# Expert loop written out without branches, and ScalarE issuing the down weights

## The chip, the cores and the metric

The kernel is one program on one core of one Trainium2 chip. The metric is the device time of one execution in microseconds (us), the median of repeated executions. The program is written instruction by instruction for each engine: TensorE (PE in the profile, PEld for its weight loads), VectorE (DVE), ScalarE (ACT), GpSimd (POOL) and SyncE (SP, which issues most transfers). Engines wait for each other and for transfers through semaphores.

## The reference, cut to what matters

A hybrid layer over 512 tokens of width 1024: a mixer (gated linear attention and dilated attention), a router, and a mixture of 32 experts, four for each token. The change touches the experts only:

```python
def expert_block(args):
    xb, e = args
    h = xb @ w_gate_up[e] + b_gate_up[e]
    gate = jnp.minimum(h[:, ::2], SWIGLU_LIMIT)
    up = jnp.clip(h[:, 1::2], -SWIGLU_LIMIT, SWIGLU_LIMIT)
    act = (up + 1.0) * (gate * jax.nn.sigmoid(SWIGLU_ALPHA * gate))
    return act @ w_down[e] + b_down[e]
```

`w_gate_up[e]` is 1024 x 2048 and `w_down[e]` is 1024 x 1024, both in float32: 8 MiB and 4 MiB for each expert, 384 MiB for all 32. The result is weighted by the router's gate, added up per token, and followed by an RMS norm.

## The kernel before, in words

The mixer and the router come first (up to about 672 us). Then the expert stage begins, the method `experts`. Each expert's weights are read once, as 12 chunks of 1 MiB: 8 chunks of gate and up weights (q = 0 to 7), then 4 chunks of down weights (q = 8 to 11). The chunks lie in a ring of 16 buffers (`expert_chunk` and `expert_chunk_late` in the trace). Chunk c goes to buffer c % 16, and it is issued once chunk c - 16 has been used up: PE adds 1 to the semaphore `used` after each chunk, and the issuing engine waits for `used` >= c - 15. PE waits for a chunk's own semaphore before it multiplies (`chunk_here`, L1745).

The stage works in bodies. Body e does, in this order on PE: the gate/up products of expert e+1 (8 chunks, L1915), with the turning (transposing) of expert e's activations after chunks 2 and 3 (L1888), and then the down products of expert e (4 chunks, L1924), with the turning of the gathered rows of expert e+2 (L1878) and its bias products (L1908) after the second of them. While PE does the down products, VectorE makes the activations of expert e+1 from PSUM (`swiglu`, L2001 to L2011) and ScalarE the sigmoid (L1972). ScalarE also copies turned rows and activations back (L1895, L1900), and at the end of a body writes the weighted output rows (`rows_out`, L1981). GpSimd scatters those rows to memory with an adding indirect DMA (L1870) and gathers the rows of expert e+2 (L1796). The output rows wait for the scatter of the body before.

There are 31 bodies (e = 0 to 30). Two stand before a hardware loop, 28 are in it (7 turns of 4 bodies), and one stands after it. Every engine runs this same structure:

```python
        def over_bodies(engine, body):
            for e0 in range(PEELED):
                body(engine, e0, 0)
            with engine.Fori(0, TURNS) as i:
                for u in range(self.UNROLL):
                    body(engine, PEELED + u, i)
            for e0 in range(PEELED + self.UNROLL * TURNS, LAST):
                body(engine, e0, 0)
```

A turn of the loop has 48 chunks, three times around the ring; semaphore targets and expert numbers in the loop are computed from the turn's number. SyncE issues all 12 chunks of each body in order (`load_chunk`, L1743), and after the first down chunk the three small transfers of a later expert's bias rows (L1737). After the last body, PE does the down products of expert 31 on their own (L1932), whose chunks are 380 to 383.

Of the kernel before, what the change touches and what calls it, by code (L numbers as in the profile page):

```python
# [9 lines left out]
F32R = mybir.dt.float32r  # L10
I32 = mybir.dt.int32
# [5 lines left out]
P = 128  # L17
# [29 lines left out]
N_EXPERTS, TOP_K, FF = 32, 4, D_MODEL  # L47
# [79 lines left out]
class Kernel:  # L127
# [23 lines left out]
    def build(self):  # L151
        nc = self.nc
        with ExitStack() as top:
# [33 lines left out]
            with ExitStack() as late:  # L187
# [7 lines left out]
                with ExitStack() as moe:  # L195
# [11 lines left out]
                    first = [self.sb(moe, f"expert_chunk{j}", [P, 2, self.WIDE]) for j in range(self.GU)]  # L207
# [13 lines left out]
                    self.bias_place = self.sb(moe, "bias_place_r", [P, P], F32R)  # L221
                    self.index = [self.sb(moe, f"row_index{u}", [P, 1], I32) for u in range(self.UNROLL)]
                    self.piece_row = [self.sb(moe, f"piece_row{u}", [P, self.GROUPS], I32) for u in range(self.UNROLL)]
                    self.piece_weight = [self.sb(moe, f"piece_weight{u}", [P, self.GROUPS]) for u in range(self.UNROLL)]
                    self.moe = {n: self.sem("moe_" + n) for n in (
# [1489 lines left out]
    RING = 16  # L1715
    GU, PER_BODY, UNROLL = 8, 12, 4
    PER_TURN = PER_BODY * UNROLL
    PARTS, GROUPS = P // QUARTER, FIRST_SLOTS // QUARTER
# [102 lines left out]
    def experts(self, stack):  # L1821
        nc, t = self.nc, self.t
        E, GU, BODY, TURN, RING = N_EXPERTS, self.GU, self.PER_BODY, self.PER_TURN, self.RING
        G, PARTS, PIECE, Q = self.GROUPS, self.PARTS, self.PIECE, QUARTER
# [79 lines left out]

        def gate_up_bias(pe, e0, i=0):
            pe.wait_ge(self.bias_in[e0 % 2], 16 * G * (self.UNROLL // 2) * i + 16 * G * (e0 // 2 + 1))
            for j, bank in enumerate(h_banks):
                pe.matmul(bank, self.bias_place[part_rows(j), :], self.bias_rows[e0 % 2][part_rows(j), :].bitcast(F32R),  # L1908
                          start=True, stop=False)

        def gate_up_chunk(pe, c, i, k, x=xT):
            w = chunk_here(pe, c, i)
# [6 lines left out]
        def down_chunk(pe, c, i, q):  # L1919
            w = chunk_here(pe, c, i)  # L1920
# [14 lines left out]

        def body_pe(pe, e0, i):
            e, more = i * self.UNROLL + e0, e0 < E - 2
            for q in range(BODY):
                c = self.body_chunk(e0, q)
                if q == 0:  # L1940
                    pe.wait_ge(S["x_out"], 2 * e + 4)
                    if e0 == 0:
                        pe.wait_ge(S["gu"], 2)
                        gate_up_bias(pe, 1)
                if q < GU:
                    gate_up_chunk(pe, c, i, q)
                else:
                    if q == GU:
                        pe.wait_ge(S["aT_out"], G * e + G)
                        if e0:  # L1950
                            pe.wait_ge(S["y_out"], G * e)
                    if q == BODY - 2 and e0 == E - 2:
                        turn_act(pe, E - 1, range(2))
                    if q == BODY - 1 and e0 == E - 2:
                        turn_act(pe, E - 1, range(2, G))
                    down_chunk(pe, c, i, q - GU)
                if q == 2:
                    turn_act(pe, e, range(2))
                if q == 3:
                    turn_act(pe, e, range(2, G))  # L1960
                if q == 9 and more:
                    turn_rows(pe, e + 2)
                    pe.wait_ge(S["gu"], 2 * e + 4)
                    gate_up_bias(pe, e0 + 2, i)

# [7 lines left out]

        def rows_out(act, e0, i):
            e = i * self.UNROLL + e0
            act.wait_ge(S["used"], TURN * i + self.body_chunk(e0, BODY - 1) + 1)
            act.wait_ge(S["pieces"], 2 * e + 2)
            if e0:
                act.wait_ge(S["scattered"], 16 * G * e)
            for j in range(G):  # L1980
                act.activation(y[:, j * PIECE:(j + 1) * PIECE], y_of(j), ACT.Copy,  # L1981
                               scale=self.piece_weight[e0 % self.UNROLL][:, j:j + 1]).then_inc(S["y_out"], 1)
# [13 lines left out]
        def swiglu(dve, e, c, i, first=False):  # L1996
            dve.wait_ge(S["used"], TURN * i + c + 1)
            if not first:
# [13 lines left out]

        def body_dve(dve, e0, i):
            e, more = i * self.UNROLL + e0, e0 < E - 2
            if more:
                u = (e0 + 2) % self.UNROLL
                if e0 > 1:
# [5 lines left out]
            swiglu(dve, e + 1, self.body_chunk(e0, GU - 1), i)  # L2023

# [45 lines left out]

        with nc.Block() as block:
            @block.sync
            def _(sp):
# [8 lines left out]

                def body(sp, e0, i):
                    e = i * self.UNROLL + e0
                    for q in range(BODY):
                        c = self.body_chunk(e0, q)
# [29 lines left out]
            def _(pool):  # L2116
# [20 lines left out]

                def body(pool, e0, i):
                    e = i * self.UNROLL + e0
                    if e0 < E - 2:  # L2140
                        gather(pool, e + 2, (e0 + 2) % self.UNROLL)
                    scatter(pool, e, e0 % self.UNROLL)
                over_bodies(pool, body)
# [29 lines left out]
            def _(dve):  # L2173
# [4 lines left out]
                dve.wait_ge(self.normed_stored, 16 * NB)  # L2178
                swiglu(dve, 0, GU - 1, 0, first=True)
                dve.wait_ge(S["lists_in"], 16 * (1 + PARTS))  # L2180
# [36 lines left out]
            def _(pe):  # L2217
# [9 lines left out]
                for c in range(GU):  # L2227
                    gate_up_chunk(pe, c, 0, c, as_rows(aT))
                    if c == 5:
# [288 lines left out]
```

## Time and profile before

| what | us |
|---|---|
| median of 3 runs | 1821.0 (1819.9 to 1821.1) |
| profiled execution, its own time | 1832.81 |
| span of the profiled execution | 1831.0 |
| PE busy in that span | 1767.4 (97%) |
| VectorE, ScalarE, GpSimd busy | 449.8, 378.9, 218.1 |
| one body without a pause (881.02 to 914.60) | 33.58 |

The profiled execution is 11.8 us longer than the median run, so a sum made from the trace is set against 1832.81 first and brought to the median afterwards. A row of the timeline gives the start, the time of the whole group, the engine and line, what is written from what, how many records, and in brackets how long the engine was idle before it and what ended that. "issue" means that the profile shows nothing the engine waited for.

### The profile page before, as it was taken

To read this page: it belongs to the slowest core of one execution; us is meant where nothing else is said; L and a number is where in the kernel's file an instruction comes from. 1 tells how busy PE (TensorE), PEld (TensorE's weight loads), DVE (VectorE), ACT (ScalarE), POOL (GpSimd) and SP (SyncE) were. 2 spreads that over 40 slices of the span, in tenths; PEclk is the share of its full clock that TensorE was granted. 3 is DMA by queue.
4 is the path that set the end of the run, shared out by engine and by line. 5 is a ranking of instruction groups with operands and counts; after the bars stand their busy time and mean duration, and the time that the engine had idled before them with its cause. 6 is when DMAs were issued, how large, how long until landed. Compare 5 with 4: busy or idle time off the path is not lost.

```text
span 1831.0 us, 38017 instructions
## 1 busy us (share of the span) xinstructions
PE 1767.4 (97%) x16447; PEld 996.1 (54%) x16448; DVE 449.8 (25%) x692; ACT 378.9 (21%) x673; POOL 218.1 (12%) x182
## 2 busy tenths in 40 slices
PE   9999999999999989999999989989999989989997
PEld 7877788898888863433433433434334334334433
DVE  4256255446324540100100100100010001001003
ACT  4254232246422321110101111111111101101111
POOL 1000000000000013121112112112111211211111
PEclk9999999999999989999999999999999999999999
DMA  5321344412223787999989999999999999999973
GB/s 186 123 92 47 120 139 116 122 40 100 92 92 138 270 329 288 384 388 398 394 321 395 394 338 386 397 334 375 397 347 389 389 343 381 392 344 382 397 276 100
DMA packets 112158, 500.47 MB, mean 273 GB/s; under 512 B 19512, under 2 KB 29712, under 8 KB 62400
## 3 DMA queue, kind: packets, MB, share of 16 engines
q1 hardware_dynamic: 92272, 479.12, 68.4%
q0 software_dynamic: 18672, 16.74, 4.5%
q10 hardware_dynamic: 1056, 2.16, 0.5%
q8 instruction: 140, 2.29, 0.5%
q14 instruction: 18, 0.15, 0.0%
HBM read 486.07 MB, written 21.15 MB: 277 GB/s over the span
## 4 chain that ended last, share of the span: by engine, by line
PE 61%; issue 2%; DVE 0%; POOL 0%; ACT 0%; DVEq 0%
PE psum L1915 38%; PE psum L1924 18%; PE psum L1888 2%; PE psum L1878 1%; PE psum L1908 1%; PE psum L1932 1%; PE psum L244 0%; DVE expert_chunk L2056 0%; DVE h_sb L2212 0%; POOL total_rstd L2147 0%; PE psum L2045 0%; PE psum L2039 0%; ACT up_values L2168 0%; DVE gate_values L2212 0%; PE psum L2237 0%
## 5 line engine op out<-in xcount | busy, mean ns | idle before, releaser
L1915 PE MATMUL psum<-expert_chunk,rowsT 128*32 128x512 f32 x2976 | 341.9, 611 | 30.7 <-issue 30.7
L1915 PE MATMUL psum<-expert_chunk_late,rowsT 128*32 128x512 f32 x2976 | 328.5, 593 | 0.0
L2001 DVE TENSOR_SCALAR gate_values<-psum 128x768 f32<-128x768 f32 x32 | 30.6, 958 | 974.9 <-PE psum L1915 974.9
L1870 POOL DMA_INDIRECT residual_rows<-h_sb,piece_row x93 | 145.4, 1564 | 903.9 <-ACT h_sb L1981 830.0
L1915 PEld LDWEIGHTS psum<-expert_chunk,rowsT 128*32 128x32 f32 x2976 | 97.1, 112 | 243.9 <-issue 242.2
L1915 PEld LDWEIGHTS psum<-expert_chunk_late,rowsT 128*32 128x32 f32 x2976 | 93.4, 110 | 202.9 <-issue 200.5
L290 DVE TENSOR_TENSOR chunk_lo<-chunk,chunk_hi 128x2048 fp32r<-128x2048 f32 x48 | 110.0, 2291 | 257.5 <-ACT chunk_hi L286 238.7
L1924 PE MATMUL psum<-expert_chunk_late,activationsT 128*32 128x256 f32 x3072 | 172.2, 380 | 0.0
L1924 PE MATMUL psum<-expert_chunk,activationsT 128*32 128x256 f32 x2880 | 161.3, 380 | 0.0
L321 PE MATMUL psum<-xT_hi,chunk_hi 128*128 128x512 f32 x384 | 150.3, 392 | 4.5 <-DVE chunk_lo L290 2.0
L321 PE MATMUL psum<-xT_hi,chunk_lo 128*128 128x512 f32 x384 | 149.5, 389 | 0.0
L321 PE MATMUL psum<-xT_lo,chunk_hi 128*128 128x512 f32 x384 | 149.5, 389 | 0.0
L1924 PEld LDWEIGHTS psum<-expert_chunk_late,activationsT 128*32 128x32 f32 x3072 | 98.1, 110 | 73.8 <-issue 13.6
L286 ACT CAST chunk_hi<-chunk 128x2048 fp32r<-128x2048 f32 x48 | 91.8, 1913 | 189.5 <-PE psum L321 158.0
L1924 PEld LDWEIGHTS psum<-expert_chunk,activationsT 128*32 128x32 f32 x2880 | 92.1, 110 | 69.3 <-issue 12.6
L321 PE MATMUL psum<-chunk_hi,xT_hi 128*128 128x512 f32 x288 | 113.5, 394 | 2.6 <-ACT gla_v L723 1.5
L321 PE MATMUL psum<-chunk_hi,xT_lo 128*128 128x512 f32 x288 | 112.7, 391 | 0.0
L321 PE MATMUL psum<-chunk_lo,xT_hi 128*128 128x512 f32 x288 | 112.6, 391 | 0.0
L1900 ACT COPY activationsT<-psum 128x256 f32<-128x256 f32 x93 | 31.6, 374 | 338.6 <-PE psum L1888 305.0
L1972 ACT ACTIVATE gate_sigmoid<-gate_values 128x768 f32<-128x768 f32 x32 | 27.1, 847 | 350.0 <-DVE gate_values L2001 350.0
L321 PEld LDWEIGHTS psum<-xT_hi,chunk_hi 128*128 128x128 f32 x384 | 72.1, 188 | 21.3 <-DVE chunk_lo L290 2.7
L321 PEld LDWEIGHTS psum<-xT_hi,chunk_lo 128*128 128x128 f32 x384 | 72.1, 188 | 15.2
(281 smaller groups left out, 1533.1 us busy)
## 6 DMA issues: line engine op xcount, KB each, us to landing
expert_chunk<-in_expert_w_gate_up SPq DMA_DIRECT2D x132, 1024.0 KB
expert_chunk_late<-in_expert_w_gate_up SPq DMA_DIRECT2D x124, 1024.0 KB, 8.3
expert_chunk_late<-in_expert_w_down SPq DMA_DIRECT2D x68, 1024.0 KB, 8.1
expert_chunk<-in_expert_w_down SPq DMA_DIRECT2D x60, 1024.0 KB
chunk<-in_w_in SPq DMA_DIRECT2D x38, 1024.0 KB, 5.1
chunk<-in_w_branch_gla SPq DMA_DIRECT2D x4, 1024.0 KB, 5.1
chunk<-in_w_mix_out SPq DMA_DIRECT2D x4, 1024.0 KB, 5.1
gla_v<-in_x SPq DMA_DIRECT2D x4, 512.0 KB
```

The source lines that it names most:

```text
L286: act.copy(self.whi[c][:], self.raw[c][:]).then_inc(self.hi_done[c], 1)
L290: dve.tensor_tensor(self.wlo[c][:], self.raw[c][:], self.whi[c][:].bitcast(F32), ALU.subtract).then_inc(self.lo_done[c], 1)
L321: last = pe.matmul(bank, stationary, moving, start=(k == 0 and n == 0), stop=(k == KT - 1 and n == 2))
L1870: pool.indirect_dma_start(pieces, bass.IndirectOffsetOnAxis(ap=self.piece_row[u][:, j:j + 1], axis=0), y[:, j * PIECE:(j + 1) * PIECE], No ...
L1878: last = pe.transpose(turned(f)[:, k, :], rows[taken, (HALF_KT * f + k) * P:(HALF_KT * f + k + 1) * P], self.ident[taken, taken])
L1888: last = pe.transpose(turned_act(j)[:, k * P:(k + 1) * P], a[:, (2 * j + k) * P:(2 * j + k + 1) * P], self.ident[:])
L1900: act.copy(dst[:, :, :, part_rows(j)].rearrange("p q k r -> p k q r"), turned_act(j).rearrange("p (k q r) -> p k q r", k=2, q=PARTS)).then ...
L1908: pe.matmul(bank, self.bias_place[part_rows(j), :], self.bias_rows[e0 % 2][part_rows(j), :].bitcast(F32R), start=True, stop=False)
L1915: last = pe.matmul(bank[part_rows(p), :], x[:, k, part_rows(j)], w[:, p // 2, p % 2 * COLS:(p % 2 + 1) * COLS], start=False, stop=(k == KT ...
L1924: last = pe.matmul(y_of(j)[part_rows(p), :], aT[:, q, kk, part_rows(j)], w[:, kk, p * PIECE:(p + 1) * PIECE], start=(q == 0 and kk == 0), ...
L1972: act.activation(sg[:, 0:HELD], gv[:, 0:HELD], ACT.Sigmoid, scale=SWIGLU_ALPHA).then_inc(S["sig"], 1)
L2001: dve.tensor_scalar(by_row(gv), gates_ups[:, :, :, :, 0], SWIGLU_LIMIT, None, ALU.min).then_inc(S["gu"], 1)
```

## The change

The loop over the bodies is written out for all engines: no loop instruction, no branch, and all semaphore targets and expert numbers are constants. Four buffers of the small index tables stay four. In addition, the down chunks of each expert but expert 0 are issued by ScalarE, in its own DMA queue, instead of SyncE: in body e ScalarE issues the four down chunks of expert e+1, after the sigmoid of expert e+1 and before it copies the turned rows back. The four waits for free ring buffers are kept, before each transfer. SyncE keeps the gate/up chunks, the bias rows and the four down chunks of expert 0.

```diff
-    def chunk_here(self, pe, c, i=0):
-        pe.wait_ge(self.chunk_loaded[c % self.RING], 16 * (self.PER_TURN // self.RING) * i + 16 * (c // self.RING + 1))
+    def chunk_here(self, pe, c):
+        pe.wait_ge(self.chunk_loaded[c % self.RING], 16 * (c // self.RING + 1))
         return self.expert_ring[c % self.RING]
...
-        def body_act(act, e0, i):
-            e = i * self.UNROLL + e0
+        def body_act(act, e):
             act_back(act, e, aT)
             gate_sigmoid(act, e + 1)
-            if e0 < E - 2:
+            for q in range(BODY - GU):
+                c = self.body_chunk(e + 1, GU + q if e + 1 < LAST else q)
+                act.wait_ge(S["used"], c - RING + 1)
+                self.load_down(act, c, e + 1, q)
+            if e < E - 2:
                 rows_back(act, e + 2, xT)
             else:
                 act_back(act, E - 1, as_act(xT))
-            rows_out(act, e0, i)
+            rows_out(act, e)
...
-        PEELED, LAST = 2, E - 1
-        TURNS = (LAST - PEELED) // self.UNROLL
+        LAST = E - 1
 
         def over_bodies(engine, body):
-            for e0 in range(PEELED):
-                body(engine, e0, 0)
-            with engine.Fori(0, TURNS) as i:
-                for u in range(self.UNROLL):
-                    body(engine, PEELED + u, i)
-            for e0 in range(PEELED + self.UNROLL * TURNS, LAST):
-                body(engine, e0, 0)
+            for e in range(LAST):
+                body(engine, e)
...
-                def body(sp, e0, i):
-                    e = i * self.UNROLL + e0
+                def body(sp, e):
                     for q in range(BODY):
-                        c = self.body_chunk(e0, q)
-                        if c < RING:
-                            continue
-                        sp.wait_ge(S["used"], TURN * i + c - RING + 1)
-                        if q < GU:
-                            self.load_gate_up(sp, c, e + 1, q)
-                        else:
-                            self.load_down(sp, c, e, q - GU)
-                        if q == GU and e0 < E - 2:
-                            self.load_bias_rows(sp, e + 2, e0)
+                        c = self.body_chunk(e, q)
+                        if c >= RING and (q < GU or e == 0):
+                            sp.wait_ge(S["used"], c - RING + 1)
+                            if q < GU:
+                                self.load_gate_up(sp, c, e + 1, q)
+                            else:
+                                self.load_down(sp, c, e, q - GU)
+                        if q == GU and e < E - 2:
+                            self.load_bias_rows(sp, e + 2, e)
                 over_bodies(sp, body)
-                for q in range(4):
-                    c = self.body_chunk(LAST, q)
-                    sp.wait_ge(S["used"], c - RING + 1)
-                    self.load_down(sp, c, LAST, q)
```

The other bodies (`body_pe`, `body_dve`, GpSimd's) lose the turn's number in the same way and keep their instructions and their order.

## Rows read from the trace of the kernel before

**Rows 1.** The page, part 1: busy time, share of the span, instructions.

```profile
PE 1767.4 (97%) x16447; PEld 996.1 (54%) x16448; DVE 449.8 (25%) x692; ACT 378.9 (21%) x673; POOL 218.1 (12%) x182
```

**Rows 2.** Waits of PE, 713 to 1800 us: total, times, longest.

```profile
PE psum L1915 <- issue: 30.7, 7, 6.3
```

**Rows 3.** Timeline of PE around the loop's turns.

```profile
780.30 7.91 PE L1915 MATMUL psum<-expert_chunk,rowsT 128*32 128x512 f32 x72
788.14 0.66 PE L1888 MATMUL psum<-identity_sb,h_sb 128*128 128x128 f32 x4
...
909.39 5.39 PE L1924 MATMUL psum<-expert_chunk_late,activationsT 128*32 128x256 f32 x96
919.84 10.63 PE L1915 MATMUL psum<-expert_chunk,rowsT 128*32 128x512 f32 x72 [5.06 <-issue]
...
1638.90 0.66 PE L1888 MATMUL psum<-identity_sb,h_sb 128*128 128x128 f32 x4
...
1765.34 7.91 PE L1915 MATMUL psum<-expert_chunk,rowsT 128*32 128x512 f32 x72
1773.18 0.66 PE L1888 MATMUL psum<-identity_sb,h_sb 128*128 128x128 f32 x4
```

**Rows 4.** Windows: busy us (records) of each engine, granted clock, DMA share, GB/s.

```profile
919.84:930.40 10.56, 10.56 (x73) 2.75 (x73) 0.00 (x0) 0.00 (x0) 3.28 (x3) 0.74 0.64 172
```

**Rows 5.** The same view, one body without a pause, one with it, one late.

```profile
881.02:914.60 33.58, 33.58 (x405) 13.54 (x397) 3.95 (x7) 3.93 (x9) 5.75 (x4) 1.00 1.01 388
914.60:948.20 33.60, 28.54 (x274) 9.54 (x274) 3.30 (x4) 3.07 (x7) 5.75 (x4) 0.90 0.87 304
...
1698.20:1731.77 33.57, 33.57 (x405) 13.67 (x401) 3.95 (x7) 3.93 (x9) 5.75 (x4) 1.00 1.02 399
```

**Rows 6.** DMA queues, 914 to 926 us: packets, MB, share of 16 engines.

```profile
q8 instruction: 3, 0.05, 1.6%
```

**Rows 7.** DMA queues, 1117 to 1130 us.

```profile
q8 instruction: 1, 0.02, 0.5%
q0 software_dynamic: 6, 0.00, 0.0%
```

**Rows 8.** Waits of SP's queue, 713 to 1800 us.

```profile
SPq L1743 <- PE psum L1915: 521.5, 236, 10.6
SPq L1743 <- PE psum L1924: 282.2, 120, 3.6
```

**Rows 9.** Chunks of expert_chunk_late, 748 to 781 us: issue to landing.

```profile
DMA to landing us min/median/max: 8.6/8.7/8.9
```

**Rows 10.** The same, 882 to 910 us.

```profile
DMA to landing us min/median/max: 8.4/8.5/8.6
```

**Rows 11.** Timeline of all engines in one body, 1100 to 1140 us.

```profile
1111.87 0.33 SPq L1743 DMA_DIRECT2D expert_chunk<-in_expert_w_down  x1
...
1120.46 0.84 ACT L1972 ACTIVATE gate_sigmoid<-gate_values 128x768 f32<-128x768 f32 x1 [11.09 <-DVE gate_values L2001]
...
1125.09 0.86 ACT L1895 COPY rowsT<-psum 128x384 f32<-128x384 f32 x2 [3.79 <-PE psum L1878]
...
1130.95 7.91 PE L1915 MATMUL psum<-expert_chunk_late,rowsT 128*32 128x512 f32 x72
```

**Rows 12.** DMA instructions in ScalarE's queue (L1110): count, duration ns min/median/max.

```profile
L1110 ACTq DMA_DIRECT2D qk_halves_then_probsT<-att_kT x16: 631/672/769, 304.6 to 331.3; - x16
L1110 ACTq DMA_DIRECT2D qk_halves_then_probsT<-att_qT_window x8: 632/1131/1732, 215.7 to 223.9; - x8
```

**Rows 13.** Timeline of PE, 1620 to 1831 us: the end of the stage.

```profile
1798.88 13.97 PE L1932 MATMUL psum<-expert_chunk_late,rowsT 128*96 128x512 f32 x32
```

**Rows 14.** Timeline of ACT, 1720 to 1831 us.

```profile
1788.42 0.85 ACT L1972 ACTIVATE gate_sigmoid<-gate_values 128x768 f32<-128x768 f32 x1 [11.09 <-DVE gate_values L2001]
1792.94 0.65 ACT L1900 COPY rowsT<-psum 128x256 f32<-128x256 f32 x2 [3.67 <-PE psum L1888]
```

**Rows 15.** DMA issues by line: count, KB each, median us to landing.

```profile
chunk<-in_w_in SPq DMA_DIRECT2D x38, 1024.0 KB, 5.1
```

More of the change, by code:

```diff
@@ L221, in build @@
                     self.bias_place = self.sb(moe, "bias_place_r", [P, P], F32R)
-                    self.index = [self.sb(moe, f"row_index{u}", [P, 1], I32) for u in range(self.UNROLL)]
-                    self.piece_row = [self.sb(moe, f"piece_row{u}", [P, self.GROUPS], I32) for u in range(self.UNROLL)]
-                    self.piece_weight = [self.sb(moe, f"piece_weight{u}", [P, self.GROUPS]) for u in range(self.UNROLL)]
+                    self.index = [self.sb(moe, f"row_index{u}", [P, 1], I32) for u in range(self.BUFFERS)]
+                    self.piece_row = [self.sb(moe, f"piece_row{u}", [P, self.GROUPS], I32) for u in range(self.BUFFERS)]
+                    self.piece_weight = [self.sb(moe, f"piece_weight{u}", [P, self.GROUPS]) for u in range(self.BUFFERS)]
                     self.moe = {n: self.sem("moe_" + n) for n in (
@@ L1715 @@
     RING = 16
-    GU, PER_BODY, UNROLL = 8, 12, 4
-    PER_TURN = PER_BODY * UNROLL
+    GU, PER_BODY, BUFFERS = 8, 12, 4
     PARTS, GROUPS = P // QUARTER, FIRST_SLOTS // QUARTER
@@ L1901, in act_back, with gate_up_bias, gate_up_chunk @@
                          turned_act(j).rearrange("p (k q r) -> p k q r", k=2, q=PARTS)).then_inc(S["aT_out"], 1)
-        def gate_up_bias(pe, e0, i=0):
-            pe.wait_ge(self.bias_in[e0 % 2], 16 * G * (self.UNROLL // 2) * i + 16 * G * (e0 // 2 + 1))
+        def gate_up_bias(pe, e):
+            pe.wait_ge(self.bias_in[e % 2], 16 * G * (e // 2 + 1))
             for j, bank in enumerate(h_banks):
-                pe.matmul(bank, self.bias_place[part_rows(j), :], self.bias_rows[e0 % 2][part_rows(j), :].bitcast(F32R),
+                pe.matmul(bank, self.bias_place[part_rows(j), :], self.bias_rows[e % 2][part_rows(j), :].bitcast(F32R),
                           start=True, stop=False)
-        def gate_up_chunk(pe, c, i, k, x=xT):
-            w = chunk_here(pe, c, i)
+        def gate_up_chunk(pe, c, k, x=xT):
+            w = chunk_here(pe, c)
             for j, bank in enumerate(h_banks):
@@ L1917, in gate_up_chunk, with down_chunk @@
             last.then_inc(S["used"], 1)
-        def down_chunk(pe, c, i, q):
-            w = chunk_here(pe, c, i)
+        def down_chunk(pe, c, q):
+            w = chunk_here(pe, c)
             for kk in range(2):
@@ L1934, in last_down_chunk, with body_pe @@
             last.then_inc(S["used"], 1)
-        def body_pe(pe, e0, i):
-            e, more = i * self.UNROLL + e0, e0 < E - 2
+        def body_pe(pe, e):
+            more = e < E - 2
             for q in range(BODY):
-                c = self.body_chunk(e0, q)
+                c = self.body_chunk(e, q)
                 if q == 0:
                     pe.wait_ge(S["x_out"], 2 * e + 4)
-                    if e0 == 0:
+                    if e == 0:
                         pe.wait_ge(S["gu"], 2)
@@ L1945, in body_pe @@
                 if q < GU:
-                    gate_up_chunk(pe, c, i, q)
+                    gate_up_chunk(pe, c, q)
                 else:
@@ L1949, in body_pe @@
                         pe.wait_ge(S["aT_out"], G * e + G)
-                        if e0:
+                        if e:
                             pe.wait_ge(S["y_out"], G * e)
-                    if q == BODY - 2 and e0 == E - 2:
+                    if q == BODY - 2 and e == E - 2:
                         turn_act(pe, E - 1, range(2))
-                    if q == BODY - 1 and e0 == E - 2:
+                    if q == BODY - 1 and e == E - 2:
                         turn_act(pe, E - 1, range(2, G))
-                    down_chunk(pe, c, i, q - GU)
+                    down_chunk(pe, c, q - GU)
                 if q == 2:
@@ L1963, in body_pe @@
                     pe.wait_ge(S["gu"], 2 * e + 4)
-                    gate_up_bias(pe, e0 + 2, i)
+                    gate_up_bias(pe, e + 2)
         def gate_sigmoid(act, e, first=False):
@@ L1972, in gate_sigmoid, with rows_out @@
             act.activation(sg[:, 0:HELD], gv[:, 0:HELD], ACT.Sigmoid, scale=SWIGLU_ALPHA).then_inc(S["sig"], 1)
-        def rows_out(act, e0, i):
-            e = i * self.UNROLL + e0
-            act.wait_ge(S["used"], TURN * i + self.body_chunk(e0, BODY - 1) + 1)
+        def rows_out(act, e):
+            act.wait_ge(S["used"], self.body_chunk(e, BODY - 1) + 1)
             act.wait_ge(S["pieces"], 2 * e + 2)
-            if e0:
+            if e:
                 act.wait_ge(S["scattered"], 16 * G * e)
@@ L1991, in body_act, with swiglu @@
                 act_back(act, E - 1, as_act(xT))
-            rows_out(act, e0, i)
-        def swiglu(dve, e, c, i, first=False):
-            dve.wait_ge(S["used"], TURN * i + c + 1)
+            rows_out(act, e)
+        def swiglu(dve, e, c, first=False):
+            dve.wait_ge(S["used"], c + 1)
             if not first:
@@ L2011, in swiglu, with body_dve @@
             dve.tensor_tensor(a[:, 0:HELD], uv[:, 0:HELD], sg[:, 0:HELD], ALU.mult).then_inc(S["act"], 1)
-        def body_dve(dve, e0, i):
-            e, more = i * self.UNROLL + e0, e0 < E - 2
+        def body_dve(dve, e):
+            more = e < E - 2
             if more:
-                u = (e0 + 2) % self.UNROLL
-                if e0 > 1:
+                u = (e + 2) % self.BUFFERS
+                if e > 1:
                     dve.wait_ge(S["scattered"], 16 * G * (e - 1))
@@ L2022, in body_dve @@
                 list_hot(dve, E - 1)
-            swiglu(dve, e + 1, self.body_chunk(e0, GU - 1), i)
+            swiglu(dve, e + 1, self.body_chunk(e, GU - 1))
         def further_experts(dve):
@@ L2136, in _, with body @@
                                    ).then_inc(S["lists_in"], 16)
[L2138 to L2142, printed above, removed]
+                def body(pool, e):
+                    if e < E - 2:
+                        gather(pool, e + 2, (e + 2) % self.BUFFERS)
+                    scatter(pool, e, e % self.BUFFERS)
                 over_bodies(pool, body)
@@ L2178, in _ @@
                 dve.wait_ge(self.normed_stored, 16 * NB)
-                swiglu(dve, 0, GU - 1, 0, first=True)
+                swiglu(dve, 0, GU - 1, first=True)
                 dve.wait_ge(S["lists_in"], 16 * (1 + PARTS))
@@ L2227, in _ @@
                 for c in range(GU):
-                    gate_up_chunk(pe, c, 0, c, as_rows(aT))
+                    gate_up_chunk(pe, c, c, as_rows(aT))
                     if c == 5:
```

7 lines of the change are left out of this document (3 added, 4 removed).

## The prediction

> **What bounds the kernel now.** I read the page first: PE is busy 97% of the span [rows 1], so only PE's idle time and slow time are to be won. The list of PE's waits over the expert stage then shows what there is: 30.7 us in seven waits, all before L1915 and all put down to "issue", a wait for nothing the profile shows [rows 2]. The timeline of PE says where. A body starts at 780.30 with no idle time, but the first products of the second turn start 5.06 us after the end of the last ones, and 72 products then take 10.63 us where 7.91 is normal [rows 3]. The granted clock in those 10.56 us is 0.74, a mix of 2.4 and 1.2 GHz, and it is 1.00 in a body without a pause [rows 4, 5]. PE had been idle just before. The pauses lie at the six returns from the end of the loop to its start. The first entry (780.30) and the exit (body 30, at 1765.34) have none [rows 3].
>
> Price of the pauses: the turning at L1888 in the first body of a turn is at 788.14 in the first turn and at 1638.90 in the seventh, 850.76 us later. Without a return, four bodies take 1773.18 - 1638.90 = 134.28 us, 33.57 each [rows 3]. Six turns at that pace are 805.68. The rest, **45.08 us**, is 7.5 for each return: 30.7 idle [rows 2], 14.4 in slow products.
>
> Next I asked whether transfers would take over. In bodies without a pause the DMA share is 1.01 to 1.02 at 388 to 399 GB/s; in the one with a pause 0.87 at 304 [rows 5]. So the transfer engines are full too, and get a rest only in the pauses. But SP waits before its chunk transfers, 356 times, 804 us in all, for PE to free a buffer [rows 8]; PE's seven waits were all at the returns. And the time from issue to landing doesn't grow from one body to those some 130 us later in the same turn: 8.7, then 8.5 us [rows 9, 10]. A need above 33.57 us of transfer for each body would add up there. PE bounds, transfers come within about 1%.
>
> **The loop written out.** PE keeps every product and order; only the returns go. What is left between two bodies is what stands between the bodies inside a turn: nothing. The terms are -30.7 idle, and -14.4 for the clock, since PE is no longer idle before it. Sum -45.1. All other engines lose their returns too; they wait for PE, so 0. The constants in place of registers on SP save nothing, as SP waits for PE anyway [rows 8].
>
> The mechanism I assume is fetching instructions: three packets of the instruction queue in the 12 us around a return, against one in 13 us in mid-body [rows 6, 7]. Written out, PE reads the same number of instructions in sequence, as it does inside a turn, which is 134 us without a pause. "Advanced Engine Details and Errata" of the Trainium skill, section Control Flow Timing, gives a jump 51 ns and a compare-and-jump 108 ns: by it six returns would cost 0.65 us at most and the time would be about 1820.4. "Runtime: NRT & Kernel Launch" of the Trainium skill, section Instruction fetch mechanics, says that a taken branch out of a small window must first fetch its target. The traced 5 us idle speaks for the second page.
>
> **ScalarE's transfers.** Four DMA instructions a body enter between the sigmoid, which ends at 1121.30, and the copy of the turned rows at 1125.09, before which ScalarE is idle 3.79 us [rows 11]. The nearest rows for one such instruction in its queue are 0.672 us (median) and, at worst, 1.73 [rows 12]. Four take 2.7 us: hidden in the 3.79. At the worst they take 6.9: the copy then ends at 1129.1, and PE needs it at 1130.95 [rows 11]. The four waits for `used` ask for chunks 4 to 7 of the body, which the sigmoid's own wait already implies, so they hold nothing up: 0. In the last body the sigmoid ends at 1789.27 and the next copy starts at 1792.94 [rows 14]: 2.7 fits, 6.9 is 3.3 too late. So 0, with +3.3 as the other end; the median row is nearest.
>
> **Later transfers.** The first of the four was issued at 1111.87 [rows 11] and will be at 1121.3: 9.4 us later, the others less. A chunk is issued 15 chunks of PE work ahead of its use, 15/12 x 33.57 = 42.0 us. Less 8.7 of landing [rows 9] and 9.4 of lateness leaves 24 us. The four come in one burst while SP goes on with its own; the work for the transfer engines stays the same, so they stay busy on a backlog instead of an even stream: 0. The gather that PE's turning waits for is over by 1117 [rows 7], ahead of the burst: 0. SP's bias transfers go out a few us sooner: 0.
>
> The last expert's down chunks are special: SP has them long ready, now they are issued from 1789.3 on. PE wants the first at 1798.88 and one every 13.97/4 = 3.5 us [rows 13]. Other chunks are done by then, so landing takes between 5.1 us, a lone chunk in the mixer [rows 15], and 8.7 [rows 9]: with 0.7 for the instruction, 1795.1 to 1798.7. Each further MiB at 390 GB/s is 2.7 us, faster than PE. So 0; with an instruction of 1.73 us and the long landing, +0.9.
>
> **Sum.** Against the profiled execution's own time: 1832.81 - 45.1 = 1787.7. Its distance of 11.8 us to the median isn't placed by any row; I let it stay: 1821.0 - 45.1 = **1776**. If all 11.8 us sat in the pauses, unprofiled runs would lose only 33.3 and come to 1787.7.
>
> **Rivals.**
>
> *Transfers become the bound, in part.* For: the share of 1.02, no rest any more, two hardware queues at once for over 1000 us, which no row shows. Against: no growth of landing in four bodies. If two queues served together raise a body's need by x us over 33.57, the 24 us of lead are eaten first, then PE waits: 31x - 24. At x = 1.5 (throughput down 4%) this is 22.5 us lost and 1798.
>
> *Transfers bound it outright (the slow side).* Same place, larger x: at 31x - 24 = 45, x = 2.2, a loss of 6% in GB/s, the gain is gone. At 10% a body needs 37.3 us: 91.6 lost, 1867. "DMA: Bandwidth & Descriptors" of the Trainium skill, section Queues, rings and completion order, says that each transfer engine takes turns between the queues that have work, a packet at a time; by it throughput would hold, and only the chunks would land in another order. No row here shows two loaded hardware queues.
>
> *The pause isn't the jump's.* Something else that comes each fourth body, such as the ring's third time around, stays: 1821. Against: no pause at the entry nor at the exit.
>
> *The pauses are shorter without a profile:* 1783 to 1788, as above.
>
> **How the numbers follow.** Forecast as worked out, 1770 to 1783: 0.64. Pauses shorter, 1783 to 1788: 0.10. Transfers in part, 1776 to 1818: 0.14, half of it above 1797. Not the jump: 0.04. Slow side: 0.08. The range 1769 to 1797 leaves out 0.07 + 0.04 + 0.08 = 0.19; its low end allows for some us of gain from code that lies differently in memory, as no row excludes it. The measurement can tell about 0.2% from no change. Faster is 0.64 + 0.10 + 0.14 = 0.88, same 0.04, slower 0.08.
>
> **What would show it.** Right: PE has no idle time of over 1 us between two bodies from 713 us to the last, 33.57 us for each of them, granted clock 1.00, and the stage ends 45 us sooner. ScalarE's DMA instructions total under 3.8 us a body, and its copy of rows still waits for PE. Landing times rise from 8.5 us toward 15 for chunks that meet a burst, and SP still waits for PE. Wrong: pauses of PE at chunk waits, at q = 8 or in gate/up chunks of late experts, with GB/s below 388 in full windows; or "issue" pauses that come back in written-out code; or a wait of PE before L1932 for the last four chunks.

## Result and the profile after

The changed kernel takes 1778.9 us (median of 4 runs, 1778.25 to 1779.55), the kernel before 1820.45 (1819.14 to 1821.1): a ratio of 0.9773, 95% interval 0.9756 to 0.979. That is 41.6 us less; 45.1 less and 1776 were forecast. A later comparison (experiment 10) gave 1778.6 against 1821.9, ratio 0.9761 (0.9747 to 0.9774). The profiled execution took 1779.54 us, with a span of 1777.7.

The page of the kernel after: lines of parts 1, 3 and 5 (the costliest product groups). They answer to [rows 1] and [rows 2]. Lines moved by one or two: L1914 is the gate/up product, L1923 the down product, L1887 the turning of activations, L1742 the chunk transfer.

```profile
span 1777.7 us, 36227 instructions
PE 1748.5 (98%) x16447; PEld 991.6 (56%) x16448; DVE 449.9 (25%) x692; ACT 379.0 (21%) x673; POOL 218.2 (12%) x182
...
q1 hardware_dynamic: 74416, 349.09, 50.4%
q10 hardware_dynamic: 18912, 132.20, 18.8%
...
L1914 PE MATMUL psum<-expert_chunk,rowsT 128*32 128x512 f32 x2976 | 328.6, 593 | 0.0
L1914 PE MATMUL psum<-expert_chunk_late,rowsT 128*32 128x512 f32 x2976 | 328.5, 593 | 0.0
```

From the page of the kernel before:

```profile
q10 hardware_dynamic: 1056, 2.16, 0.5%
...
L1915 PE MATMUL psum<-expert_chunk,rowsT 128*32 128x512 f32 x2976 | 341.9, 611 | 30.7 <-issue 30.7
```

PE has the same number of products as before. The 30.7 us of idle time before L1914 are now 0.0. The group that starts each turn of the loop, on `expert_chunk`, lost 13.3 us of busy time (341.9 before, 328.6 now) and is as fast as its twin on the late buffers. Queue q10 is ScalarE's: it carries 132 MB where it carried 2.16 before, and q1 carries 130 MB less.

The timeline of PE in the kernel after, from the first expert to the last products of the stage. It answers to [rows 3] and [rows 13].

```profile
687.39 7.93 PE L1914 MATMUL psum<-expert_chunk,activationsT 128*32 128x512 f32 x72
695.25 0.88 PE L1877 MATMUL psum<-identity_sb,h_sb 96*128 96x96 f32 x8
...
711.81 0.66 PE L1887 MATMUL psum<-identity_sb,h_sb 128*128 128x128 f32 x4
...
1738.29 0.66 PE L1887 MATMUL psum<-identity_sb,h_sb 128*128 128x128 f32 x4
...
1744.70 13.97 PE L1931 MATMUL psum<-expert_chunk_late,rowsT 128*96 128x512 f32 x32
```

These two turnings at L1887 (of expert 0's activations in the first body, and of expert 31's among the last body's down products) are my marks: each run below is measured between them, and the distance of neighbouring marks is one body. Here they are 1026.48 us apart. No row between them has an idle time in brackets. The list of PE's waits over this stretch is empty.

The same two marks in the kernel before, and its first expert ahead of them:

```profile
687.27 7.56 PE L1915 MATMUL psum<-expert_chunk,activationsT 128*32 128x512 f32 x63
695.22 1.08 PE L1915 MATMUL psum<-expert_chunk,activationsT 128*32 128x512 f32 x5 [0.38 <-issue]
...
700.20 0.64 PE L1878 MATMUL psum<-identity_sb,h_sb 96*128 96x96 f32 x3 [1.63 <-issue]
...
720.99 0.66 PE L1888 MATMUL psum<-identity_sb,h_sb 128*128 128x128 f32 x4
...
1792.47 0.66 PE L1888 MATMUL psum<-identity_sb,h_sb 128*128 128x128 f32 x4
```

Here the marks are 1071.48 us apart, so the stage is 45.0 us shorter, as worked out. But the span is 53.3 us shorter. The rest comes from before the first mark, which is at 711.81 instead of 720.99, 9.2 us sooner; behind the last mark the kernel after takes 0.9 us longer. In the profiled execution of the kernel before, PE crawls through the first expert between 695 and 702 us, a few products at a time with "issue" between them; in the kernel after it doesn't. The change adds and removes no product in this stretch, and experiment 6 will show the same crawl in written-out code.

ScalarE's timeline in one body after, and landing times of the late buffers between 748 and 781 and between 1600 and 1700 us. They answer to [rows 11] and [rows 9, 10].

```profile
1129.92 0.85 ACT L1971 ACTIVATE gate_sigmoid<-gate_values 128x768 f32<-128x768 f32 x1 [11.09 <-DVE gate_values L2002]
1129.92 2.59 ACTq L1742 DMA_DIRECT2D expert_chunk_late<-in_expert_w_down  x4
1134.56 0.86 ACT L1894 COPY rowsT<-psum 128x384 f32<-128x384 f32 x2 [3.79 <-PE psum L1877]
```

```profile
DMA to landing us min/median/max: 4.8/13.3/18.3
...
DMA to landing us min/median/max: 5.2/14.3/18.2
```

The four transfers take 2.59 us together (2.1 to 3.5 over the 31 bodies, 2.59 in the mean), starting with the sigmoid, and the copy that follows still waits for PE, 3.79 us as before. The median landing takes 13.3 us between 748 and 781 us, where it was 8.7, and 14.3 between 1600 and 1700, where it was 8.5:

```profile
DMA to landing us min/median/max: 8.1/8.5/10.1
```

### The profile page after: what moved, and what is told of

The parts are those of the page before. It is cut to its first block, busy times and chain, and to the rows that moved or that the text cites. A ratio compares the mean times of both kernels' runs of the same rounds, so it can differ in the third digit from the quotient of the medians.

```text
span 1777.7 us, 36227 instructions
## 1 busy us (share of the span) xinstructions
PE 1748.5 (98%) x16447; PEld 991.6 (56%) x16448; DVE 449.9 (25%) x692; ACT 379.0 (21%) x673; POOL 218.2 (12%) x182
## 4 chain that ended last, share of the span: by engine, by line
PE 61%; DVE 0%; POOL 0%; ACT 0%; issue 0%; DVEq 0%
PE psum L1914 38%; PE psum L1923 18%; PE psum L1887 2%; PE psum L1877 1%; PE psum L1907 1%; PE psum L1931 1%; PE psum L244 0%; DVE expert_chunk L2057 0%; DVE h_sb L2200 0%; POOL total_rstd L2135 0%; PE psum L2046 0%; PE psum L2040 0%; ACT up_values L2156 0%; DVE gate_values L2200 0%; PE psum L2225 0%; PE psum L1758 0%
## 5 line engine op out<-in xcount | busy, mean ns | idle before, releaser
L1914 PE MATMUL psum<-expert_chunk,rowsT 128*32 128x512 f32 x2976 | 328.6, 593 | 0.0
L1914 PE MATMUL psum<-expert_chunk_late,rowsT 128*32 128x512 f32 x2976 | 328.5, 593 | 0.0
L1914 PEld LDWEIGHTS psum<-expert_chunk_late,rowsT 128*32 128x32 f32 x2976 | 93.4, 110 | 202.9 <-issue 200.5
L1914 PEld LDWEIGHTS psum<-expert_chunk,rowsT 128*32 128x32 f32 x2976 | 93.5, 110 | 202.4 <-issue 199.7
L1923 PE MATMUL psum<-expert_chunk_late,activationsT 128*32 128x256 f32 x3072 | 172.2, 380 | 0.0
L1923 PE MATMUL psum<-expert_chunk,activationsT 128*32 128x256 f32 x2880 | 161.3, 380 | 0.0
L1923 PEld LDWEIGHTS psum<-expert_chunk_late,activationsT 128*32 128x32 f32 x3072 | 98.1, 110 | 73.9 <-issue 13.6
L1923 PEld LDWEIGHTS psum<-expert_chunk,activationsT 128*32 128x32 f32 x2880 | 92.1, 110 | 69.3 <-issue 12.7
L321 PEld LDWEIGHTS psum<-xT_hi,chunk_lo 128*128 128x128 f32 x384 | 72.4, 189 | 15.2
```

The lines of the kernel that those rows point to most:

```text
L321: last = pe.matmul(bank, stationary, moving, start=(k == 0 and n == 0), stop=(k == KT - 1 and n == 2))
```

## Experiments

### 1 and 2: one half of the change at a time

Written out, with SyncE issuing everything (the changed kernel without ScalarE's part):

```diff
-            for q in range(BODY - GU):
-                c = self.body_chunk(e + 1, GU + q if e + 1 < LAST else q)
-                act.wait_ge(S["used"], c - RING + 1)
-                self.load_down(act, c, e + 1, q)
...
-                        if c >= RING and (q < GU or e == 0):
+                        if c >= RING:
```

> The loop is written out, but SyncE issues all chunks in order, as in the kernel before. Theory (all of the gain is PE's returns to the loop's start; the second queue is worth 0): 1779 us, equal to the changed kernel's 1778.9 within 2 us, no pause of PE, landing flat near 8.5 us. Rival (the second queue brings part of the gain, since with the share of the transfer engines at 1.02 one queue alone can't feed PE once the rests in the pauses are gone): clearly above 1785 us, with waits of PE for chunks late in the stage and landing times that grow beyond 9 us.

1777.3 us (5 runs), ratio to the kernel before 0.9757 (0.9744 to 0.9771). The whole gain is there without the second queue. From the first mark to the last there are 1026.47 us. The rival falls on time, but not on the landing times, which do grow; "landing flat near 8.5 us" was a miss. The late buffers' lines at 748 to 781, 1300 to 1400 and 1600 to 1700 us:

```profile
DMA to landing us min/median/max: 6.7/8.4/8.7
...
DMA to landing us min/median/max: 8.9/11.0/12.0
...
DMA to landing us min/median/max: 10.8/12.4/13.8
```

That is 4 us in some 26 bodies, or 0.15 us a body. This trace grows most: the same kernel in experiment 11 goes from 8.2 to 10.4 us over the same stretches (below), and experiment 3 from 8.0 to 10.2, which is 0.08 us a body.

```profile
DMA to landing us min/median/max: 6.7/8.2/8.4
...
DMA to landing us min/median/max: 8.4/10.4/11.2
```

So a body needs some 0.1 us more of transfer than PE's 33.57. In a turn of four bodies that is 0.3 to 0.6 us, too little for what I looked at in [rows 9, 10].

Experiment 2 keeps the loop and lets ScalarE issue the down chunks (SyncE leaves them out, apart from expert 0's):

```diff
             gate_sigmoid(act, e + 1)
+            for q in range(BODY - GU):
+                c = self.body_chunk(e0 + 1, GU + q if e0 + 1 < LAST else q)
+                act.wait_ge(S["used"], TURN * i + c - RING + 1)
+                self.load_down(act, c, e + 1, q)
```

> The loop of four bodies is kept on all engines, and ScalarE issues the down chunks in its own queue. Theory: 1820 us, the six pauses of 7 to 8 us each are still there, and the second queue changes nothing: ratio to the kernel before 0.998 to 1.002. Rival (the second queue is part of the gain): below 1815 us.

1836.0 us, ratio 1.0085 (1.0071 to 1.01): 15.2 us slower than the kernel before. Neither theory had that. PE's waits and one return:

```profile
PE psum L1915 <- issue: 37.9, 12, 5.2
```

```profile
900.76 5.39 PE L1924 MATMUL psum<-expert_chunk_late,activationsT 128*32 128x256 f32 x96
911.35 3.65 PE L1915 MATMUL psum<-expert_chunk,rowsT 128*32 128x512 f32 x17 [5.20 <-issue]
916.82 6.21 PE L1915 MATMUL psum<-expert_chunk,rowsT 128*32 128x512 f32 x55 [1.82 <-issue]
922.97 0.66 PE L1888 MATMUL psum<-identity_sb,h_sb 128*128 128x128 f32 x4
```

Each return now has a second pause, always after 17 products. The kernel before has one too, 0.19 us long, at its sixth return (1632.76), which is the seventh wait of [rows 2]; experiment 4 has one of 1.03 us. By the marks the six returns cost 9.2, 11.0, 8.7, 8.9, 9.2 and 9.9 us, 56.9 together instead of 45.1. The windows from the pause on show what is different: busy times, granted clock, DMA share and GB/s, first of this kernel, then of the kernel before, whose second line is [rows 4].

```profile
906.30:911.30 5.00, 0.00 (x0) 0.00 (x0) 0.00 (x0) 1.20 (x3) 2.55 (x2) 0.93 1.00 418
911.35:922.97 11.62, 9.80 (x73) 2.86 (x73) 0.00 (x0) 0.00 (x0) 3.15 (x3) 0.88 1.03 375
```

```profile
914.80:919.80 5.00, 0.00 (x0) 0.00 (x0) 0.00 (x0) 1.20 (x3) 2.43 (x2) 0.87 1.00 394
```

Before, the transfer engines ran dry soon after the pause (0.64, 172 GB/s, while PE fetched on). With the down chunks issued later and in a burst, they stay full (1.03, 375 GB/s). That suggested a theory: PE's instructions come through the same engines, and wait there for the weights. Experiments 5 and 12 test it.

### 3 and 4: whose return it is

Only PE written out, then only PE looped (there the first added line reads `is not`); SyncE issues everything:

```diff
         def over_bodies(engine, body):
+            if engine is nc.tensor:
+                for e in range(LAST):
+                    body(engine, e, 0)
+                return
             for e0 in range(PEELED):
                 body(engine, e0, 0)
```

> Only PE's program is written out; SyncE, ScalarE, VectorE and GpSimd keep the loop, and SyncE issues all chunks. Theory (PE pauses for its own jump, the jumps of the others are covered): 1779 us. Rival (the pause is made by another engine's return, by a transfer that SyncE issues late, or by five engines that fetch instructions at once): 1800 us or more, with pauses still at every fourth body.

> The reverse: PE keeps its loop, the other four engines are written out, and SyncE issues all chunks. Theory: 1820 us, six pauses of 7 to 8 us. Rival (five engines fetching at once make the pause long): pauses of 2 to 3 us and below 1800 us.

PE alone written out: 1778.7 us, ratio 0.9765 (0.9752 to 0.9779), no wait of PE in the stage. PE alone looped: 1820.6 us, ratio 1.0001 (0.9991 to 1.0011). PE's own return makes the whole difference; the other engines' returns are covered, and they don't make PE's longer. In the fourth kernel's trace:

```profile
PE psum L1915 <- issue: 29.3, 7, 5.0
```

Its six returns cost 7.3, 7.8, 6.6, 8.0, 6.8 and 8.0 us by the marks, 44.5 together.

### 5: the loop with thin transfers

The kernel leaves out three quarters of every chunk from chunk 16 on (`QUARTER * 8` is 256 of 1024 columns), so it doesn't compute the layer; its products keep their number and shape.

```diff
         r = c % self.RING
+        if c >= self.RING:
+            sp.dma_start(self.expert_ring[r][:, :, 0:QUARTER * 8], src[:, :, 0:QUARTER * 8]).then_inc(self.chunk_loaded[r], 16)
+            return
```

> The loop of four bodies is kept and SyncE issues all chunks, but from chunk 16 on only a quarter of each chunk (256 of 1024 columns) is loaded; the products run over what lay in the rest of the buffer. So the transfer engines are mostly idle at the returns. Theory (what PE waits for at a return is a packet of instructions, which has to take its turn among the weight packets in the same transfer engines): the idle time at a return falls from 5 us to 2 to 3 us, six returns cost 20 to 30 us instead of 45, and the time is 1795 to 1808 us. Rival (the return costs the same whatever the engines move): idle 5 us at each, 1820 us.

This and the next three runs were made on another chip, on which the kernel before takes 1831.7 us. The thin loop takes 1816.2, ratio 0.9924 (0.9907 to 0.994). That is 15.5 us less; 12 to 25 less were expected (1795 to 1808 against 1820), so the saving is near the weak end, and the absolute time is outside, by the chip. The six returns cost 27.3 us by the marks instead of 45. One of them, and the idle window before it:

```profile
1056.66 9.54 PE L1918 MATMUL psum<-expert_chunk,rowsT 128*32 128x512 f32 x72 [3.20 <-issue]
```

```profile
1053.46:1056.66 3.20, 0.00 (x1) 0.01 (x1) 0.00 (x0) 1.20 (x3) 0.91 (x1) 0.90 0.28 90
1056.66:1066.20 9.54, 9.54 (x73) 3.92 (x74) 0.00 (x0) 0.00 (x0) 4.84 (x4) 0.86 0.54 112
```

The pause is 2.5 to 3.2 us where it was 4.5 to 6.3. In the mean of six returns the idle time falls from 5.1 to 2.9 us. So some 2 us of it were the loaded engines, and some 3 us stay with nearly empty ones. The slow products after it stay as well: 9.54 us at a granted clock of 0.86.

### 6: six near jumps

```diff
         def body_pe(pe, e):
             more = e < E - 2
+            if e >= 6 and e % 4 == 2 and e < 30:
+                with pe.Fori(0, 2) as again:
+                    pe.sem_inc(S["cleared"], 1)
```

> Written out, SyncE issues all chunks, and PE has a loop of two turns over one semaphore instruction in front of bodies 6, 10, 14, 18, 22 and 26, the places where the loop's returns were. So six jumps back are taken, each to a target a few instructions away. Theory (the distance of the target is what costs, since it must be fetched anew): under 1 us for each, 1777 to 1782 us, no idle time of PE over 1 us. Rival (any jump that is taken empties PE and costs 5 us): six pauses, about 1820 us.

1788.2 us on the slower chip, ratio 0.9769 (0.975 to 0.9787), the ratio of the kernels without any loop. PE has no wait in the stage, and the marks are 1026.48 us apart. The place where the first of the six stands:

```profile
908.90 5.39 PE L1923 MATMUL psum<-expert_chunk_late,activationsT 128*32 128x256 f32 x96
914.10 6.19 PE L1914 MATMUL psum<-expert_chunk,rowsT 128*32 128x512 f32 x56
```

The products start with no idle time behind it. The loops did run: the trace has the records of PE's branch instructions, which the views leave out. Here they are twelve, six taken of 0.21 to 0.22 us and six not taken of 0.08, and PE reaches each while earlier products still run. In the kernel before, the six taken ones last 5.56 to 7.37 us, from 913.42 to 919.56 at the first return, and the seventh, at the exit from the loop, 0.08. So it isn't the jump as such that costs, but the far target. From what distance on it costs was not measured: the near targets are a few instructions away, the far ones four bodies of 405 products.

### 7: two returns

```diff
-        PEELED, LAST = 2, E - 1
+        PEELED, LAST = 18, E - 1
```

> The loop is kept but starts later: 18 bodies are written out ahead of it, it has 3 turns of 4 bodies, so two returns instead of six, and one body follows. SyncE issues all chunks. Theory (each return costs 7 to 7.5 us, entry and exit nothing): 1777.3 + 2 x 7.3 = 1792 us, two pauses. Rival (the entry, the mere presence of the loop, or the registers cost too): 1798 us or more.

1803.3 us on the slower chip, ratio 0.9851 (0.9835 to 0.9866). The comparison there is with experiment 6, which has no far return and took 1788.2: 15.1 us for two, where 14.6 were worked out. PE's waits:

```profile
PE psum L1915 <- issue: 9.7, 2, 4.9
```

By the marks the two returns cost 7.8 and 6.7 us, 14.5 together. That leaves 0.6 us, less than the scatter, for entry, exit and all else.

### 8 and 9: more load on the transfer engines

Both kernels are written out. In the eighth SyncE issues all chunks; the ninth is the changed kernel, with ScalarE's queue. Both get the same addition:

```diff
                     for q in range(BODY):
+                        if q == 4 and e >= 2:
+                            sp.dma_start(self.more[e], t["expert_w_gate_up"][0][e, 0:P, :]).then_inc(self.more_in, 16)
```

`self.more` is a scratch tensor in memory; SyncE waits for the copies at the very end.

> Written out, SyncE issues all chunks, and in 29 bodies it also copies 1 MiB from memory to memory that nothing waits for until the end: 2.5 us more of work for the transfer engines in each body of 33.57 us. Theory (the transfer engines are within about 1% of being the bound, with 33 us of lead in the ring): the surplus of some 2.2 us adds up to 64 us over 29 bodies, 33 are taken from the lead, and PE waits the other 31: about 1808 us, with landing times that grow from 8 us to over 40. Rival (a share of 1.02 doesn't mean full, there are several per cent of room): 1777 to 1780 us, landing times below 15 us.

> The changed kernel (ScalarE issues the down chunks) with the same additional copy of 1 MiB in 29 bodies as in the run before this one, issued by SyncE. There PE first had to wait for a chunk in the 17th body and lost 25 us. Theory (the later burst of down chunks takes 9 us of the lead, the work for the transfer engines is the same): the first wait comes some 4 to 5 bodies sooner, each body after that loses the same 1.9 us, and about 9 us more are lost: 33 to 37 us over the changed kernel on the same chip. Rival (two loaded queues need more time for the same bytes): each late body loses over 2.5 us, 45 us or more over the changed kernel. Other rival (two queues move more): under 20 us.

Eight: 1813.5 us, ratio 0.9907 (0.9886 to 0.9928), which is 25.3 over experiment 6 on that chip; 31 were expected. Nine, on the third chip: 1816.3 us, ratio 0.9969 (0.9957 to 0.9981), 37.7 over the changed kernel there (experiment 10); 33 to 37 were expected. The first waits of PE, in the eighth and then in the ninth:

```profile
1294.10 2.78 PE L1916 MATMUL psum<-expert_chunk_late,rowsT 128*32 128x512 f32 x24 [0.83 <-DMA expert_chunk_late<-in_expert_w_gate_up]
```

```profile
1054.80 5.58 PE L1916 MATMUL psum<-expert_chunk,rowsT 128*32 128x512 f32 x48 [0.17 <-DMA expert_chunk<-in_expert_w_gate_up]
```

Now PE waits for chunks, and from there on in every body. With SyncE alone that begins in the 18th body and the stage is 25.9 us longer by the marks, 1.85 for each of the last 14 bodies. With ScalarE's queue it begins in the 11th, and the stage is 38.4 longer, 1.83 for each of the last 21. The loss per body is the same, so two loaded queues carry neither more nor less than one. What differs is the lead. By my estimate, 29 copies at 1.84 us are 53.4, of which 27.5 went into the lead with SyncE alone and 15.0 with ScalarE's queue. The median landing in the ninth grows from 13.0 us (748 to 781) to 38.2 (1600 to 1700); the eighth's trace gives no landing times, so "over 40" can't be answered there. The windows of the two at the same place:

```profile
1500.00:1600.00 100.00, 95.37 (x1119) 36.78 (x1115) 11.85 (x21) 10.60 (x24) 14.77 (x11) 1.00 1.01 400
```

```profile
1500.00:1600.00 100.00, 94.48 (x1087) 36.18 (x1079) 11.84 (x21) 10.28 (x24) 16.94 (x12) 1.00 1.01 399
```

### 10 and 11: the two written-out versions side by side

> The changed kernel once more, on the same chip as the next run. Theory: within 0.2% of the version in which SyncE issues all chunks; the 1.6 us between them in two separate comparisons were scatter. Rival (the second queue costs something at the start of the stage): 1 to 3 us above it.

> Written out, SyncE issues all chunks: the same kernel as the first experiment, beside the changed one. Theory: within 0.2% of it. Rival: 1 to 3 us below it.

1778.6 us (ratio 0.9761, 0.9747 to 0.9774) and 1779.7 us (0.9767, 0.9753 to 0.978), 5 runs each on one chip. They can't be told apart, and their order is the reverse of that in experiment 1, so its 1.6 us look like scatter. No version found here beats the changed kernel.

### 12: thin transfers with both queues

The edits of experiments 2 and 5 together; this kernel leaves out the same three quarters of the chunks.

> The loop is kept and ScalarE issues the down chunks, but from chunk 16 on only a quarter of each chunk is loaded, so the products run over what lay in the rest of the buffer. With whole chunks this loop cost 57 us at its six returns instead of 45, with thin chunks issued by SyncE 27 us. Theory (the backlog of two loaded queues at the return is what made the returns dearer): 27 us again, the same time as the thin version issued by SyncE, ratio to the kernel before 0.990 to 0.995. Rival (ScalarE's own return, with transfers issued after it, makes the pause longer): 35 us or more, ratio above 0.996.

1805.0 us, ratio 0.9905 (0.9887 to 0.9923). The six returns cost 28.2 us by the marks, where they cost 27.3 with SyncE's thin chunks and 56.9 with full chunks in two queues. One of them:

```profile
906.97 9.52 PE L1918 MATMUL psum<-expert_chunk,rowsT 128*32 128x512 f32 x72 [2.50 <-issue]
```

With little in the queues, the queue that issues makes next to no difference. So the 12 us that ScalarE's queue added to the loop's returns came from the load in the transfer engines at the return, not from ScalarE's own jump.

The traces' records of single packets show how. Queue q8, which the page calls "instruction", moves packets of 16384 bytes. The table gives, for all six returns of each kernel, how long PE's branch lasts, when in it the first such packet starts, and how much later the next one does.

| kernel | branch, us | first packet, us after the branch's start | next packet, us after the first |
|---|---|---|---|
| before | 5.56 to 7.37 | 3.2 to 5.0 | 3.5 to 4.6 |
| 2, full chunks, two queues | 5.95 to 6.32 | 3.6 to 3.9 | 5.6 to 6.6 |
| 5, thin chunks, one queue | 3.55 to 4.23 | 1.2 to 1.9 | 3.0 to 3.1 |
| 12, thin chunks, two queues | 3.58 to 4.15 | 1.3 to 1.6 | 3.0 to 3.5 |

In all 24 the branch ends 2.3 to 2.7 us after the first packet inside it starts: PE waits for that packet, and the packet starts sooner where the queues hold little. In experiment 2 the branch is no longer than before (6.21 against 6.16 us in the mean). It is the next packet that comes some 2 us later, which makes the second pause; six times 2 us are the 12. The records don't name the engine that a packet is for, but with PE alone looped (experiment 4) a packet lies in each branch in the same way, 2.9 to 3.7 us behind its start.

## Why the prediction was right, step by step

**The loop written out, -45.1 us.** Place and mechanism hold. The pauses are PE's own (3 and 4), in proportion to the returns (7), with entry and exit free, and made by the far target (6), whose instructions PE waits for (12). The size held for the profiled execution: the marks are 45.0 us closer. Against the medians it is 41.6, and 43.5 against experiment 1's and 43.3 against experiment 10's, so the term is 1.6 to 3.5 us too large for the typical execution. The price of a return differs within one trace (6.2 to 8.6 us), so it may differ from execution to execution. The scatter on the first experiments' chip fits that: 1816.5 to 1824.3 us before and 1818.3 to 1823.7 with only PE looped, against 1775.6 to 1779.3 in experiments 1 and 3. But it speaks weakly, for experiment 6, without far returns, runs from 1785.3 to 1791.3. I haven't shown it.

**The clock part, -14.4.** Right: the group's products went from 341.9 to 328.6 us, 13.3 less. The other 1.1 us are ends that overlap: without a pause, a body's first product starts 0.19 us before the modelled end of the one ahead of it (914.10 against 908.90 + 5.39 in experiment 6), and six returns lose that.

**ScalarE's transfers, 0.** Right. Four take 2.59 us in the mean where 2.7 were worked out, and the copy behind them starts no later.

**Later transfers, 0.** Right in time. Landing rose to 14 us as forecast, and SyncE still waits for PE (233 times, 864.5 us). The lead, put at 24 us with ScalarE's queue and 33 without, comes out at 15.0 and 27.5 us from experiments 9 and 8: I had it too large by 6 to 9. In the changed kernel it was never used up. The last expert's down chunks came in time; L1931 starts right behind the products before it.

**Transfers "within about 1%".** Nearer than that, and on the other side: in experiments 1, 3 and 11 a body's transfers need slightly more than PE's time, and the ring's lead pays for it over all 31 bodies, 2 to 4 us of 27. So "PE bounds" held because the stage ends before the lead does. My argument for room, equal landing times in one turn, looked at too short a stretch. In the kernel before landing stays flat to the end (8.5 us from 1600 to 1700), which fits pauses that give the engines a rest.

**The 11.8 us between the profiled execution and the median.** I let them stay as an unplaced distance. They are no cost of the profile: the changed kernel's profiled execution took 1779.54 us beside a median of 1778.9. 9.2 of them lie in the first expert, around 695 to 702 us: by so much the first mark comes later than in the kernel after. The first marks of experiments 5 to 8 are as late (718.9 to 721.6 us, against 709.3 to 712.4 in all other traces but that of the kernel before), on a chip where the kernel before takes 1831.7 us. On which chip the profile of the kernel before was taken isn't on record. What makes PE slow there stays open; the windows only say that the transfer engines weren't busy (DMA share 0.60 in 688 to 704 us, against 1.02 in the kernel after):

```profile
688.00:704.00 16.00, 12.08 (x82) 3.80 (x78) 0.00 (x0) 0.04 (x1) 10.76 (x11) 0.88 0.60 211
```

One row of the crawl in experiment 6, whose code has no far return:

```profile
699.95 0.41 PE L1877 MATMUL psum<-identity_sb,h_sb 96*128 96x96 f32 x3 [1.66 <-issue]
```

**The rivals.** Two queues that cost throughput: no, by experiments 8 and 9, with 1.85 and 1.83 us a body. The rule of "DMA: Bandwidth & Descriptors" in the Trainium skill, section Queues, rings and completion order, that a transfer engine takes turns between its queues, agrees with that. Not the jump: no. "Advanced Engine Details and Errata" in the Trainium skill, section Control Flow Timing, gives a compare-and-branch 108 ns; the traces have 80 ns for one that isn't taken, 210 to 220 ns for a near one that is, and 5.6 to 7.4 us for the far ones of the kernel before. The figure is not met by any of the three, and the measurement decides. The rule of "Runtime: NRT & Kernel Launch" in the Trainium skill, section Instruction fetch mechanics, that a taken branch whose target isn't held must first fetch it, agrees with both: one instruction packet stands in each far branch, and near ones cost no time.

## What to carry to other kernels

A hardware loop with a long body can cost its engine a pause at every return, here 7.5 us on PE with the slow products behind it, for a loop of four bodies with 405 products each; count the returns, look at the first row of each turn, and write out the loop of the engine that sets the time, which may be that engine alone. When transfers run near their limit, judge their room by landing times over many bodies without a pause, since pauses give it back unseen. A second queue added no throughput here (400 and 399 GB/s); what mattered was how long ahead of its use a transfer is issued, and what else, instructions included, has to pass behind it.

## What the runs showed of the hardware that I had not expected

- A far return is one branch instruction that waits for one packet of 16 KiB in the instruction queue, and ends 2.3 to 2.7 us after that packet starts.
- The return's price depends on the load of the transfer engines: 4.6 us each with thin chunks (share 0.28 in the pause), 7.5 with one loaded queue, 9.5 with two, where the engines stay full behind the return (1.03).
- With no loop, the second queue moves the time by less than the measurement can tell; with the loop it costs 15.2 us. The two halves of this change aren't independent.
- One chip runs the kernel before and the written-out kernel 10.9 us slower than the first experiments' chip. The written-out traces differ by 11.2 us already at the first mark (720.51 against 709.33), and by nothing between the marks.
